# Prompt attention of a hybrid decoder: pairs in a new order, two sets of score buffers, and the second compression in two halves

## The chip, the cores and the metric

The kernel runs on one core of a Trainium2 chip. The metric is the device time of one execution in microseconds; the median of the runs is compared. The engines are TensorE (PE; PEld is its weight load), VectorE (DVE), ScalarE (ACT), GpSimd (POOL) and SyncE (SP); the last two mostly issue DMAs here. Each engine works through its own instructions in the order in which they are written, and waits at semaphores for the others.

## The reference, cut to what matters

Two layers of a decoder over 256 prompt tokens and 32 sample tokens (8 sequences of 4), all in f32. Each layer has three token mixers on one input projection; the change concerns the first, attention with three branches, for the prompt tokens. Keys of branch 0 are compressed: 32 positions of a stride of 16 are projected by weights `w_cmp`, for keys (kind 0) and values (kind 1).

```python
k_cmp = compress(strides[:, :, :, 0], w_halves[0])
v_cmp = compress(strides[:, :, :, 1], w_halves[1])
s_c = jnp.einsum('qgrd,cgd->qgrc', qi, k_cmp[b]) * scale      # branch 0: compressed
p_c = masked_softmax(s_c, ...);  o_c = jnp.einsum('qgrc,cgd->qgrd', p_c, v_cmp[b])
...                                                          # branch 1: selected blocks, branch 2: window, alike
o_nsa = jnp.einsum('bthk,btkhd->bthd', g_nsa, o_br)          # gated sum of the three
```

The sample tokens attend to 1024 past positions, whose rows lie in pages; these too are compressed, for the first four sequences (half 0) and the last four (half 1). After the mixers come the gated merge, an output projection, and in layer 0 a dense feed-forward network, in layer 1 a mixture of 8 experts.

## The kernel before

**Pairs.** The prompt's attention is cut into six pairs of a query tile qt (128 queries each) and a branch br. `pair_width` gives the keys: 15 for branch 0, 128 for the other branches of qt 0, and 256 for those of qt 1 (qt 1 sees both key tiles). I call a pair with 256 keys wide and the others slim. Each pair goes through the engines in this chain, for two key groups g:

- PE `pair_scores` (L633) makes the scores in PSUM, one bank for each g, two for a wide pair.
- DVE `pair_softmax` (L1573, L1577) scales and masks them into the score buffer `S_p[g]` in SBUF and takes the maximum.
- ACT `pair_exp` (L1333) takes the exponential in place, with the sum.
- DVE `pair_norm` (L1587 to L1592) multiplies by the gate over the sum.
- PE transposes (`pair_transposes`, L646), ACT copies the result from PSUM into `PT_p` (L1198, in `evac`) and gives a mark (`signal`, L1222).
- PE multiplies by the values (`pair_out`, L658), and DVE adds the result into `oN` (`pair_out`, L1600 to L1603), pair by pair.

There is one set of score buffers: `pair_softmax(m)` may write `S_p` only once the transposes of pair m-1 have read it (`filled(("T", l, m - 1, ...))`).

**What fills the chain's waits.** The input projection has 22 tiles that the attention doesn't need: `rest(i)` is one product of 8 blocks (L476), with an evacuation on ACT or DVE (kind x, c, b: a copy; z: Silu; h: a product on DVE). `PAIR_RESTS` puts nine of them, 3 to 11, between the steps of the pairs. A rest of kind z makes ACT load another function table than the exponential. `compress(1)`, the compression of half 1 of the sample's pages (L596, L603), stands in one piece before the scores of pair 3; ACT evacuates it (`evac_cmp`).

**Queues.** PSUM has 8 banks, taken in turn by every product (`bank`): PE waits until the use eight before has been evacuated. Weights come through a ring of 6 slots of 1 MB, 16 blocks each, which SP loads in the order in which PE uses them. The sample's pages are filled into three slots of `pages`, half by SP and half by POOL (`page_fill`, L435; windows of keys at L1096 and L1099), each fill when its slot's last reader is done (`frees`). PE waits in `compress` for both page fills of the half. After the pairs PE waits for `qbd`, the sample's queries spread out by DVE (L1642, L1645), and the sample's attention begins with the transposes at L681.

Of the kernel before, what the change touches and what calls it, by code (L numbers as in the profile page):

```python
# [39 lines left out]

CMP1_RESTS = 3
PAIRS = [(qt, br) for qt in range(2) for br in range(3)]
CMP1_PAIR = 2
PAIR_RESTS = [(3, 4), (5,), (6, 7), (8,), (9, 10), (11,)]

# [115 lines left out]
def build(nc, xT_in, consts, params, wstream, page_table, cmp_pages, slc_pages, win_kT, win_v, win_rows,  # L161
# [5 lines left out]
    with ExitStack() as ctx:  # L167
# [18 lines left out]
        mark = sb("mark", 2 * MARKS)  # L186
        REG = 11600
        reg = sb("phase_region", REG)
# [50 lines left out]
        rp = Region(scratch)  # L239
        S_p = [rp(1024), rp(1024)]  # L240
        PT_p = [rp(2, 4 * P), rp(2, 4 * P)]
        rs_ = Region(scratch)
        qbd = rs_(NB, 32)
        vc = rs_(HALF, P)
# [197 lines left out]
        def _(pe):  # L442
# [73 lines left out]
            for l in range(DEPTH):  # L516
# [40 lines left out]
                def rest(i):  # L557

                    product(("rest", l, i), KD, lambda k: xn[:, k, :])
# [13 lines left out]

                def compress(hf):

                    fills = [(l, hf, "cmp0"), (l, hf, "cmp1")]
                    for f in fills:
# [3 lines left out]
                        "p (n k j g c) -> p n k j g c", n=n, k=2, j=JP, g=NKV) for f, n in zip(fills, blocks_of)]  # L581
                    for kind in range(2):
                        out = [bank(("cmp", l, hf, kind, k)) for k in range(2)]
# [29 lines left out]
                for i in range(1, EARLY):  # L613
                    rest(i)
                compress(0)

# [21 lines left out]
                def pair_transposes(m):  # L638
                    w, nkc = pair_width(m)
                    for g in range(NKV):  # L640
                        s = S_p[g][:, 0:GRP * w * nkc].rearrange("p (r k) -> p r k", r=GRP)
# [546 lines left out]
        def _(act):  # L1188
# [56 lines left out]
            for l in range(DEPTH):  # L1245
# [81 lines left out]
                def pair_exp(m):  # L1327
                    w, nkc = pair_width(m)
                    for g in range(NKV):
                        s = S_p[g][:, 0:GRP * w * nkc].rearrange("p (r k) -> p r k", r=GRP)  # L1330
                        act.wait_ge(S["smax"], 12 * l + 2 * m + g + 1)
                        for r in range(GRP):
                            e = A.activation(s[:, r, :], s[:, r, :], ACT.Exp, bias=mx[:, g, r:r + 1],  # L1333
                                             accum_out=ssum[:, g, r:r + 1])
                        e.then_inc(S["exp_ready"], 1)

                pair_exp(0)
                for m in range(6):
                    w, nkc = pair_width(m)
                    if m == CMP1_PAIR:  # L1340
                        for kind, k in ((0, 0), (0, 1), (1, 0), (1, 1)):
                            evac_cmp(("cmp", l, 1, kind, k), kvT[1][kind][:, 2 * k:2 * k + 2, :])
                        signal("vcT_ready")
                    rest(PAIR_RESTS[m][0])
# [6 lines left out]
                    for i in PAIR_RESTS[m][1:]:  # L1351
                        rest(i)
# [128 lines left out]
        def _(dve):  # L1481
# [36 lines left out]
            for l in range(DEPTH):  # L1518
# [37 lines left out]
                def pair_softmax(m):  # L1556
# [9 lines left out]
                    for g in range(NKV):  # L1566
                        s = S_p[g][:, 0:GRP * w].rearrange("p (r k) -> p r k", r=GRP)
# [11 lines left out]
                def pair_norm(m):  # L1579
# [4 lines left out]
                    for g in range(NKV):  # L1584
                        s = S_p[g][:, 0:GRP * w].rearrange("p (r k) -> p r k", r=GRP)
                        dve.wait_ge(S["exp_ready"], 12 * l + 2 * m + g + 1)
                        link(V.reciprocal(rsum, ssum[:, g, :]))  # L1587
                        gate = gates[:, qt, g * 12:(g + 1) * 12].rearrange("p (r k) -> p r k", k=3)[:, :, br]
                        link(V.tensor_tensor(coef, rsum, gate, ALU.mult))
                        if br == 0:  # L1590
                            link(V.tensor_scalar(coef, coef, C("cmp_any")[:, qt:qt + 1], None, ALU.mult))
                        V.tensor_tensor(s, s, bc(coef, 2, w), ALU.mult).then_inc(S["norm_ready"], 1)  # L1592

                def pair_out(m):
# [3 lines left out]
                    dst = oN[:, :, qt * P:(qt + 1) * P]  # L1598
                    if br == 0:
                        V.tensor_copy(dst, src).then_inc(free(("O", l, m)), 1)  # L1600
                    else:
                        dve.wait_ge(*released(("O", l, m - 1)))
                        V.tensor_tensor(dst, dst, src, ALU.add).then_inc(free(("O", l, m)), 1)  # L1603
# [29 lines left out]
                for m in range(6):  # L1633
                    pair_norm(m)
                    rest(PAIR_RESTS[m][0])
                    if m < 5:
                        pair_softmax(m + 1)
                    for i in PAIR_RESTS[m][1:]:
                        rest(i)
                    pair_out(m)  # L1640

                link(V.memset(qbd, 0.0))  # L1642
                for g in range(NKV):
                    gd = slice(HD * g, HD * g + HD)
                    last = V.tensor_copy(qbd[gd, :, 16 * g:16 * g + 16].rearrange("p b (r t) -> p b r t", r=GRP),  # L1645
                                         qkv[gd, 0:GRP, TP:T].rearrange("p r (b t) -> p b r t", b=NB))
                last.then_inc(S["qbd_ready"], 1)
                for hf in range(2):
# [433 lines left out]
def weight_stream(a):  # L2082
# [9 lines left out]
    for l in range(DEPTH):  # L2092
# [10 lines left out]
        put(cm)  # L2103
        put(np.stack(rest[EARLY:EARLY + CMP1_RESTS]))
        put(cm)
        put(np.stack(rest[EARLY + CMP1_RESTS:]))
        mg = blocks(w[:, 4128:]).reshape(3, KD, KD, P, P)
# [127 lines left out]
```

## Time and profile before

| | |
|---|---|
| median of 3 runs | 2044.54 us (2044.1 to 2047.66) |
| the profiled execution | 2039.56 us, its span 2037.9 us |
| PE | busy 1973.1 us, 97% of the span |
| DVE, ACT, POOL | 463.2, 291.9 and 143.3 us |
| chain that ended last | PE 88%, issue 8%, DVE 2%, ACT 1%, DMA 1% |
| granted TensorE clock, mean | 0.991 |

PE is the engine to watch: what ends later on it ends the kernel later. The prompt's pairs run from 92.04 to 175.35 us in layer 0 and from 779.04 to 862.29 us in layer 1. The experts take the span's second part, from about 1150 us on, in which the DMA engines are nearly full. A busy PE is modelled: each matmul's shown end lies somewhat behind the start of the next, so that a row's length is longer than its place in the sequence.

### The profile page before, as it was taken

Reading aid. Unit: us, or ns where it says so; the run is one execution under the profiler, and the core shown is the slowest. Engines: PE = TensorE matmul, PEld = TensorE weight load, DVE = VectorE, ACT = ScalarE, POOL = GpSimd, SP = SyncE. Lnnn points to the kernel's source line nnn. Section 1 sums busy time; section 2 is a strip of 40 time slices with the busy share of each in tenths; the row PEclk is TensorE's granted clock in tenths of the full one; section 3 lists DMA queues with packets and bytes.
Section 4 is the critical chain, followed back from the end, with each engine's and each line's share of the span. In section 5 each row is a group of like instructions: output and inputs, shape, how many; then the busy total and the mean of one; then the engine's idle time right before and its main releaser. Section 6 shows DMA issues by size and latency. Waiting matters only on the chain.

```text
span 2037.9 us, 40320 instructions
## 1 busy us (share of the span) xinstructions
PE 1973.1 (97%) x17106; PEld 1418.3 (70%) x17106; DVE 463.2 (23%) x1189; ACT 291.9 (14%) x737; POOL 143.3 (7%) x246
## 2 busy tenths in 40 slices
PE   8998999999999999899999999999999999999996
PEld 6876677777777778667777556777767675646564
DVE  2334464310000132437442410010100100101011
ACT  2243222100000023512211200000000000000000
POOL 2210120000000010120000200000000000000000
PEclk9999999999999999999999999999999999999998
DMA  8853654364333264454233499999999999999996
GB/s 308 316 201 115 219 192 142 135 214 175 142 127 143 105 227 166 149 203 148 106 127 143 169 414 417 412 418 414 416 417 413 420 408 421 411 421 411 415 420 241
DMA packets 99833, 553.25 MB, mean 271 GB/s; under 512 B 13712, under 2 KB 30128, under 8 KB 40912
## 3 DMA queue, kind: packets, MB, share of 16 engines
q1 hardware_dynamic: 84144, 491.96, 61.1%
q0 software_dynamic: 12720, 48.97, 6.8%
q10 hardware_dynamic: 2800, 9.83, 1.4%
q8 instruction: 135, 2.21, 0.4%
q14 instruction: 34, 0.28, 0.0%
HBM read 532.08 MB, written 24.89 MB: 273 GB/s over the span
## 4 chain that ended last, share of the span: by engine, by line
PE 88%; issue 8%; DVE 2%; ACT 1%; DMA 1%; POOL 0%; DVEq 0%; POOLq 0%; SPq 0%; ACTq 0%
PE bank L476 42%; PE bank L966 35%; PE bank L603 3%; PE bank L633 1%; PE bank L658 1%; PE bank L742 1%; PE bank L720 1%; ACT phase_region L1198 0%; PE bank L786 0%; DVE phase_region L1573 0%; PE bank L854 0%; PE bank L933 0%; PE bank L646 0%; PE bank L495 0%; PE bank L487 0%
## 5 line engine op out<-in xcount | busy, mean ns | idle before, releaser
L966 PE MATMUL bank<-wring,phase_region 128*32 128x512 f32 (+2 forms) x10112 | 867.7, 506 | 1.0 <-DMA wring<-in_wstream 0.8
L966 PEld LDWEIGHTS bank<-wring,phase_region 128*32 128x32 f32 x10112 | 572.6, 110 | 296.0 <-issue 142.8
L476 PE MATMUL bank<-xn,wring 128*128 128x288 f32 x2496 | 631.5, 412 | 5.7 <-DVE phase_region L1573 3.6
L476 PEld LDWEIGHTS bank<-xn,wring 128*128 128x128 f32 x2496 | 473.1, 192 | 144.5 <-issue 12.7
L476 PE MATMUL bank<-phase_region,wring 128*128 128x288 f32 x608 | 148.2, 407 | 3.1 <-DVE mark L1494 2.5
L2046 DVE TENSOR_TENSOR tmp<-phase_region,bank 128x512 f32<-128x512 f32 (+1 forms) x48 | 28.6, 595 | 500.9 <-PE bank L966 500.9
L476 PEld LDWEIGHTS bank<-phase_region,wring 128*128 128x128 f32 x608 | 115.4, 190 | 36.0 <-DVE mark L1494 3.4
L1198 ACT ACTIVATE phase_region<-bank 128x512 f32<-128x512 f32 (+12 forms) x130 | 55.7, 469 | 411.7 <-PE bank L966 296.5
L1469 ACT ACTIVATE phase_region<-bank 128x512 f32<-128x512 f32 (+1 forms) x48 | 26.1, 544 | 531.6 <-PE bank L966 531.6
L2059 DVE COPY phase_region<-bank 32x256 f32<-32x256 f32 x32 | 13.5, 420 | 263.0 <-PE bank L966 262.7
L603 PE MATMUL bank<-pages,wring 128*64 128x128 f32 (+1 forms) x1024 | 58.9, 276 | 0.0
L603 PEld LDWEIGHTS bank<-pages,wring 128*64 128x64 f32 x1024 | 57.8, 137 | 0.0
L1174 POOL TENSOR_TENSOR turn<-turn 1x1 f32<-1x1 f32 x8 | 1.5, 183 | 678.8 <-DVE slot_row L2054 673.2
L1934 DVE TENSOR_TENSOR phase_region<-phase_region,bank 128x288 f32<-128x288 f32 x22 | 9.9, 454 | 158.7 <-PE bank L476 140.4
L435 POOL DMA_DIRECT2D pages<-in_slc_pages x64 | 34.3, 536 | 97.1 <-PE bank L603 68.7
L1573 DVE SCALAR_TENSOR_TENSOR phase_region<-bank,cst 128x512 f32<-128x512 f32 (+1 forms) x32 | 17.5, 567 | 100.3 <-PE bank L646 57.3
L435 POOL DMA_DIRECT2D pages<-in_cmp_pages x64 | 34.4, 538 | 58.1 <-issue 55.3
L1333 ACT ACTIVATE phase_region<-phase_region 128x15 f32<-128x15 f32 (+2 forms) x96 | 37.6, 392 | 3.1 <-DVE phase_region L1577 2.8
L1240 ACT ACTIVATE tmp<-xT 128x288 f32<-128x288 f32 x32 | 13.5, 440 | 160.3 <-DVE xT L1938 85.6
L1781 DVE TENSOR_TENSOR tmp<-bank,tmp 128x288 f32<-128x288 f32 x32 | 14.6, 457 | 90.4 <-PE bank L476 90.4
L1391 ACT ACTIVATE tmp<-bank 128x288 f32<-128x288 f32 x40 | 16.2, 409 | 123.6 <-PE bank L476 101.5
L1110 POOL DMA_DIRECT2D phase_region<-phase_region x16 | 7.9, 499 | 365.4 <-ACT phase_region L1255 365.4
(335 smaller groups left out, 1129.4 us busy)
## 6 DMA issues: line engine op xcount, KB each, us to landing
wring<-in_wstream SPq DMA_DIRECT2D x449, 1024.0 KB, 8.3
y_rows<-phase_region ACTq DMA_DIRECT2D x25, 384.0 KB, 7.5
pages<-in_cmp_pages POOLq DMA_DIRECT2D x64, 128.0 KB, 4.0
pages<-in_cmp_pages SPq DMA_DIRECT2D x64, 128.0 KB, 3.8
pages<-in_slc_pages SPq DMA_DIRECT2D x64, 128.0 KB, 4.4
pages<-in_slc_pages POOLq DMA_DIRECT2D x64, 128.0 KB, 4.5
out_win_keep<-in_win_rows POOLq DMA_DIRECT2D x2, 4064.0 KB, 26.4
pages<-in_win_kT POOLq DMA_DIRECT2D x4, 1024.0 KB, 5.3
```

The lines of the kernel that those rows point to most:

```text
L435: eng.dma_start(pages[:, at:at + 2 * P], src[bass.ds(page + l * n_pool, 1), :, :].rearrange("a p n -> (a p) n")).then_inc(fill_at[f][1], 16)
L476: mm = nc.tensor.matmul(ps[:, 0:width], wb, rhs(k), start=(k == 0), stop=(k == n - 1))
L603: mm = nc.tensor.matmul(ps[HD * g:HD * g + HD, 1 - a:1 - a + CPG * n].rearrange("p (n c) -> p n c", c=CPG), w, src[k][:, :, kind, jp, g, : ...
L633: mm = nc.tensor.matmul(ps[:, i * nk:(i + 1) * nk], qkv[gd, part * per + i, qt * P:qt * P + P], keys, start=True, stop=True)
L658: mm = nc.tensor.matmul(ps[gc, 0:512], v, PT_p[g][0:w, kc, :], start=(kc == 0), stop=(kc == nkc - 1))
L720: mm = nc.tensor.matmul(ps[32 * bi:32 * bi + 32, 0:512].rearrange("p (a b) -> p a b", a=4), qbd[:, hf * HALF + bi, :], kT[:, 4 * c:4 * c + ...
L742: nc.tensor.matmul(ps[32 * bi:32 * bi + 32, 0:P], PT_s[:, c, 32 * bi:32 * bi + 32], keys[bi][2][:, c, :], start=(c == 0), stop=False)
L966: mm = nc.tensor.matmul(ps[QT * q:QT * q + QT, out0:out0 + n], lhsT, wring[:, a:a + n], start=start, stop=stop)
L1198: return A.activation(out, in_, ACT.Copy)
L1333: e = A.activation(s[:, r, :], s[:, r, :], ACT.Exp, bias=mx[:, g, r:r + 1], accum_out=ssum[:, g, r:r + 1])
L1469: A.activation(sg[:, r % 3, 0:cols], psum[loop_bank(key)][:, 0:cols], ACT.Silu).then_inc(bank_free[loop_bank(key)], 1)
L2046: V.tensor_tensor(hq[r % 2][:, 0:cols], sg[:, r % 3, 0:cols], psum[b][:, 0:cols], ALU.mult).then_inc(bank_free[b], 1)
```

## The change

Four things change, all within the pairs of both layers. The order of the pairs becomes (0,0), (1,1), (0,1), (1,2), (0,2), (1,0) in (qt, br), so that pairs 1 and 3 are the wide ones. Even and odd pairs get score buffers of their own, `S_slim` and `S_wide`; `pair_softmax(m)` waits for the transposes of pair m-2. `compress(1)` is called once for each kind, behind the scores that follow pair 1's and pair 3's: kind 0 between the scores of pair 2 and the transposes of pair 1, kind 1 between the scores of pair 4 and the transposes of pair 3. There ACT takes the exponential of pair m+1 ahead of the evacuations, instead of behind them. The rests move to other places. `qbd` gets room of its own and is made after pair 0's output instead of after pair 5's. The order of the weight stream follows PE's.

```diff
-        S_p = [rp(1024), rp(1024)]
+        S_wide = [rp(1024), rp(1024)]
+        S_slim = [rp(512), rp(512)]
...
-PAIRS = [(qt, br) for qt in range(2) for br in range(3)]
-CMP1_PAIR = 2
-PAIR_RESTS = [(3, 4), (5,), (6, 7), (8,), (9, 10), (11,)]
+PAIRS = [(0, 0), (1, 1), (0, 1), (1, 2), (0, 2), (1, 0)]
+CMP1_KIND = {1: 0, 3: 1}
+BEFORE_T = [(3,), (), (), (), (8,), (10,)]
+BEFORE_O = [(4,), (5,), (6,), (7,), (9,), (11,)]
...
+        def S_p(m):
+            return S_wide if m % 2 else S_slim
...
                 for m in range(6):
-                    if m == CMP1_PAIR:
-                        compress(1)
                     if m < 5:
                         pair_scores(m + 1)
-                    rest(PAIR_RESTS[m][0])
+                    if m in CMP1_KIND:
+                        compress(1, (CMP1_KIND[m],))
+                    for i in BEFORE_T[m]:
+                        rest(i)
                     pair_transposes(m)
-                    for i in PAIR_RESTS[m][1:]:
+                    for i in BEFORE_O[m]:
                         rest(i)
                     pair_out(m)
...
-                    if m == CMP1_PAIR:
-                        for kind, k in ((0, 0), (0, 1), (1, 0), (1, 1)):
+                    if m in CMP1_KIND:
+                        pair_exp(m + 1)
+                        kind = CMP1_KIND[m]
+                        for k in range(2):
                             evac_cmp(("cmp", l, 1, kind, k), kvT[1][kind][:, 2 * k:2 * k + 2, :])
-                        signal("vcT_ready")
+                        if kind == 1:
+                            signal("vcT_ready")
...
-                    if m < 5:
+                    if m < 5 and m not in CMP1_KIND:
                         pair_exp(m + 1)
...
-                        if m:
-                            dve.wait_ge(*filled(("T", l, m - 1, g, pair_width(m - 1)[1] - 1)))
+                        if m > 1:
+                            dve.wait_ge(*filled(("T", l, m - 2, g, pair_width(m - 2)[1] - 1)))
...
                     pair_out(m)
+                    if m == 0:
+                        link(V.memset(qbd, 0.0))
```

**PE, the wide pairs before.** These are the scores of pair 4 to the last product of pair 5. L633 are scores (128x256: a wide pair), L476 a rest, L646 transposes (15x128: of a pair with 15 keys), L658 the product with the values, L681 the sample's first transposes.

```order
L633 MATMUL bank<-phase_region 128x256 x8
L476 MATMUL bank<-xn,wring 128x288 x8
L646 MATMUL bank<-cst,phase_region 15x128 x8
L658 MATMUL bank<-phase_region 64x512 x2
L633 MATMUL bank<-phase_region 128x256 x8
L476 MATMUL bank<-xn,wring 128x288 x8
L646 MATMUL bank<-cst,phase_region 128x128 x16
L476 MATMUL bank<-xn,wring 128x288 x8
L658 MATMUL bank<-phase_region 64x512 x4
L476 MATMUL bank<-xn,wring 128x288 x8
L646 MATMUL bank<-cst,phase_region 128x128 x16
L658 MATMUL bank<-phase_region 64x512 x4
```

Now PE has this from pair 1's scores to pair 2's output; L638 are the scores, L601 and L608 one kind of the compression, L651 transposes, L481 a rest and L663 the product with the values.

```order
L638 MATMUL bank<-phase_region 128x256 x8
L481 MATMUL bank<-xn,wring 128x288 x8
L651 MATMUL bank<-cst,phase_region 15x128 x8
L481 MATMUL bank<-xn,wring 128x288 x8
L663 MATMUL bank<-phase_region 64x512 x2
L638 MATMUL bank<-phase_region 128x128 x8
L601 MATMUL bank<-cst,wring 64x129 x4
L608 MATMUL bank<-pages,wring 64x128 x64
L651 MATMUL bank<-cst,phase_region 128x128 x16
L481 MATMUL bank<-xn,wring 128x288 x8
L663 MATMUL bank<-phase_region 64x512 x4
L638 MATMUL bank<-phase_region 128x256 x8
```

Between a wide pair's scores and its transposes stood one rest; now a slim pair's scores and half the compression stand there too. Between the first wide pair's output and the next transposes (those of slim pair 2) stand the scores of pair 3 alone. The first half of the compression begins one rest, one slim transpose and one slim output earlier than the whole did.

**ACT, the end of the pairs before**, from the Silu of the last rest of kind z (L1297) to the exponential of the sample's compressed scores (L1361):

```order
L1297 ACT_TABLE_LOAD
L1297 ACTIVATE o_ssm<-bank 128x288
L1198 ACTIVATE phase_region<-bank 128x512 x4
L1222 ACTIVATE mark<-cst 1x1
L1333 ACT_TABLE_LOAD
L1333 ACTIVATE phase_region<-phase_region 128x256 x8
L1198 ACTIVATE phase_region<-bank 128x288
L1198 ACTIVATE phase_region<-bank 128x512 x4
L1222 ACTIVATE mark<-cst 1x1
L1198 ACTIVATE phase_region<-bank 63x512
L1222 ACTIVATE mark<-cst 1x1
L1361 ACTIVATE phase_region<-phase_region 128x63
```

And now (L1303 is the Silu, L1371 the exponential):

```order
L1303 ACT_TABLE_LOAD
L1303 ACTIVATE o_ssm<-bank 128x288
L1204 ACTIVATE phase_region<-bank 128x288
L1204 ACTIVATE phase_region<-bank 15x512 x2
L1228 ACTIVATE mark<-cst 1x1
L1204 ACTIVATE phase_region<-bank 63x512
L1228 ACTIVATE mark<-cst 1x1
L1371 ACT_TABLE_LOAD
L1371 ACTIVATE phase_region<-phase_region 128x63
```

The last Silu stands behind the last pair's exponential, and a table load stands ahead of the exponential of the sample's scores.

## Rows read from the trace of the kernel before

**Rows 1.** PE's waits, whole span: what waited, for whom, us in total, times, longest.
```profile
PE bank L658 <- ACT mark L1222: 5.0, 6, 0.9
PE bank L476 <- DVE phase_region L1573: 3.6, 2, 1.8
PE bank L681 <- DVE phase_region L1645: 3.1, 2, 1.6
PE bank L633 <- DVE phase_region L1573: 2.0, 2, 1.0
PE bank L646 <- DVE phase_region L1573: 0.7, 2, 0.3
```
**Rows 2.** Timeline of PE, layer 0: start us, us, instructions, idle before.
```profile
104.48 1.07 PE L658 MATMUL bank<-phase_region 15*64 15x512 f32 x4
105.48 1.16 PE L633 MATMUL bank<-phase_region 64*128 64x128 f32 x16
...
133.26 1.04 PE L646 MATMUL bank<-cst,phase_region 128*128 128x128 f32 x8
134.14 4.05 PE L476 MATMUL bank<-xn,wring 128*128 128x288 f32 x16
...
139.12 2.00 PE L633 MATMUL bank<-phase_region 64*128 64x256 f32 x16
```
**Rows 3.** Timeline of DVE, layer 0, pair 0's output and pair 1's norm.
```profile
105.60 0.69 DVE L1600 COPY o_nsa<-bank 128x512 f32<-128x512 f32 x1 [2.61 <-PE bank L658]
106.21 0.17 DVE L1587 RECIPROCAL phase_region<-phase_region 128x4 f32<-128x4 f32 x1
...
107.22 0.17 DVE L1587 RECIPROCAL phase_region<-phase_region 128x4 f32<-128x4 f32 x1
```
**Rows 4.** Timeline of DVE, layer 0: wide pair 4's first softmax step and last norm step.
```profile
145.67 1.29 DVE L1573 SCALAR_TENSOR_TENSOR phase_region<-bank,cst 128x512 f32<-128x512 f32 x2 [4.14 <-PE bank L646]
...
153.22 1.23 DVE L1592 TENSOR_TENSOR phase_region<-phase_region 128x1024 f32<-128x1024 f32 x1
```
**Rows 5.** Timeline of PE: one kind of the compression (layer 0), pair 0's output (layer 1).
```profile
113.76 7.15 PE L603 MATMUL bank<-pages,wring 128*64 128x128 f32 x128
...
789.86 1.07 PE L658 MATMUL bank<-phase_region 15*64 15x512 f32 x4
```
**Rows 6.** SP's page loads of half 1, layers 0 and 1; landing time of the last.
```profile
92.88 12.16 SPq L435 DMA_DIRECT2D pages<-in_cmp_pages  x16
...
DMA to landing us min/median/max: 6.0/6.0/6.0
...
779.35 9.59 SPq L435 DMA_DIRECT2D pages<-in_cmp_pages  x16
...
DMA to landing us min/median/max: 3.4/3.9/4.5
```
**Rows 7.** Stretches: us, busy PE, PEld, DVE, ACT, POOL, granted clock, DMA share, GB/s.
```profile
156.00:160.00 4.00, 1.86 (x12) 1.23 (x10) 3.93 (x6) 3.67 (x9) 0.00 (x0) 1.00 0.00 0
...
832.00:836.00 4.00, 2.73 (x12) 1.72 (x14) 3.93 (x6) 3.58 (x11) 0.00 (x0) 0.76 0.30 119
...
1200.00:2038.00 838.00, 817.48 (x9608) 553.48 (x9600) 83.31 (x160) 35.06 (x62) 27.71 (x36) 0.99 0.99 405
```
**Rows 8.** Timeline of PE, layer 1: a wide pair's scores at the lower clock.
```profile
834.34 3.54 PE L633 MATMUL bank<-phase_region 64*128 64x256 f32 x16 [1.00 <-DVE phase_region L1573]
```
**Rows 9.** Timeline, layer 0: an ACT table load; DVE's sample probabilities, and their reader on PE.
```profile
128.77 1.28 ACT L1297 ACT_TABLE_LOAD   x1
...
177.50 0.26 DVE L1659 TENSOR_SCALAR phase_region<-phase_region 128x63 f32<-128x63 f32 x1
...
180.17 0.33 PE L692 MATMUL bank<-phase_region,cst 128*128 128x63 f32 x2
```
**Rows 10.** Timeline, layer 0: POOL's page loads of the selected blocks, their first reader.
```profile
128.81 9.32 POOL L435 DMA_DIRECT2D pages<-in_slc_pages  x16 [35.11 <-PE bank L603]
...
192.34 1.92 PE L720 MATMUL bank<-pages,phase_region 128*32 128x512 f32 x16
```

More of the change, by code:

```diff
@@ L186, in build @@
         mark = sb("mark", 2 * MARKS)
-        REG = 11600
+        REG = 11600 + 1280
         reg = sb("phase_region", REG)
@@ L239, in build @@
         rp = Region(scratch)
-        S_p = [rp(1024), rp(1024)]
+        S_wide = [rp(1024), rp(1024)]
+        S_slim = [rp(512), rp(512)]
         PT_p = [rp(2, 4 * P), rp(2, 4 * P)]
+        qbd = rp(NB, 32)
         rs_ = Region(scratch)
-        qbd = rs_(NB, 32)
         vc = rs_(HALF, P)
@@ L572, in _, with compress @@
                     nc.tensor.matmul(ps[:, 0:7 * TQ], C("spread")[:, P * r:P * r + P], qk_std, start=True, stop=True).then_inc(done, 1)
-                def compress(hf):
+                def compress(hf, kinds):
                     fills = [(l, hf, "cmp0"), (l, hf, "cmp1")]
@@ L581, in compress @@
                         "p (n k j g c) -> p n k j g c", n=n, k=2, j=JP, g=NKV) for f, n in zip(fills, blocks_of)]
-                    for kind in range(2):
+                    for kind in kinds:
                         out = [bank(("cmp", l, hf, kind, k)) for k in range(2)]
@@ L614, in _ @@
                     rest(i)
-                compress(0)
+                compress(0, (0, 1))
                 pe.wait_ge(S["vcT_ready"], 3 * l + 2)
@@ L1339, in _ @@
                     w, nkc = pair_width(m)
-                    if m == CMP1_PAIR:
-                        for kind, k in ((0, 0), (0, 1), (1, 0), (1, 1)):
+                    if m in CMP1_KIND:
+                        pair_exp(m + 1)
+                        kind = CMP1_KIND[m]
+                        for k in range(2):
                             evac_cmp(("cmp", l, 1, kind, k), kvT[1][kind][:, 2 * k:2 * k + 2, :])
-                        signal("vcT_ready")
-                    rest(PAIR_RESTS[m][0])
+                        if kind == 1:
+                            signal("vcT_ready")
+                    for i in BEFORE_T[m]:
+                        rest(i)
                     for g in range(NKV):
@@ L1348, in _ @@
                     signal("pt_ready")
-                    if m < 5:
+                    if m < 5 and m not in CMP1_KIND:
                         pair_exp(m + 1)
-                    for i in PAIR_RESTS[m][1:]:
+                    for i in BEFORE_O[m]:
                         rest(i)
@@ L1634, in _ @@
                     pair_norm(m)
-                    rest(PAIR_RESTS[m][0])
+                    for i in BEFORE_T[m]:
+                        rest(i)
                     if m < 5:
                         pair_softmax(m + 1)
-                    for i in PAIR_RESTS[m][1:]:
+                    for i in BEFORE_O[m]:
                         rest(i)
                     pair_out(m)
[L1642 to L1647, printed above, removed]
+                    if m == 0:
+                        link(V.memset(qbd, 0.0))
+                        for g in range(NKV):
+                            gd = slice(HD * g, HD * g + HD)
+                            last = V.tensor_copy(qbd[gd, :, 16 * g:16 * g + 16].rearrange("p b (r t) -> p b r t", r=GRP),
+                                                 qkv[gd, 0:GRP, TP:T].rearrange("p r (b t) -> p b r t", b=NB))
+                        last.then_inc(S["qbd_ready"], 1)
                 for hf in range(2):
@@ L2103, in weight_stream @@
         put(cm)
-        put(np.stack(rest[EARLY:EARLY + CMP1_RESTS]))
-        put(cm)
-        put(np.stack(rest[EARLY + CMP1_RESTS:]))
+        put(np.stack(rest[3:5]))
+        put(cm[0])
+        put(np.stack(rest[5:7]))
+        put(cm[1])
+        put(np.stack(rest[7:]))
         mg = blocks(w[:, 4128:]).reshape(3, KD, KD, P, P)
```

13 lines of the change are left out of this document (6 added, 7 removed).

## The prediction

> **What bounds the kernel now.** The page comes first: PE is busy 97% of the span and makes 88% of the chain that ended last. The change can gain only what PE waits, so PE's waits are read next [rows 1]. Five groups of them lie within the pairs and add up to 5.0 + 3.6 + 3.1 + 2.0 + 0.7 = 14.4 us, 7.2 in each layer. They are three things. L658 waits for ACT's mark: a pair's transposes are done and ACT still copies them, with no rest in between. L633, L476 and L646 wait for DVE at L1573: the scores of wide pair 5 can't leave PSUM, because the one set of score buffers still holds pair 4, and the products behind them find no free bank. L681 waits for L1645: the sample's queries are laid out only behind pair 5's output.
>
> A row's length overstates a group's place in the sequence, so a shown wait is too short. Slim transposes are shown at 1.04 us, and the next group starts 0.88 after them; an output is shown at 1.07, and the next starts 1.00 after it [rows 2]. Each layer has seven waits (the counts of rows 1, halved). Five follow transposes, or a part of them, and hide 0.16 each; two follow outputs and hide 0.07: 7.2 + 0.8 + 0.14 = 8.1 us of real waiting a layer.
>
> **The change part by part.** PE's instructions stay the same in number and shape; only waits change.
>
> *Removed.* The three outputs that waited for ACT's mark now have a rest of 4 us [rows 2] between transposes and output. The waits at pair 5 go: each wide pair is followed by a slim one with its own buffer. Do the wide pairs find their norm done in time? In the trace a wide pair's whole chain, from DVE's first softmax step to its last norm step, takes from 145.67 to 154.45 us, 8.8 us [rows 4]. In the new order, from the end of pair 3's scores PE passes slim transposes 0.9, rest 4, output 1.0, slim scores 1.1 and a kind of the compression of over 7.15 us [rows 2, 5] before it wants that norm: 14 us. DVE starts on pair 3 some 1 us late, behind pair 2's norm, and has pair 2's output in between: 3 us or more remain. Pair 1 has 4 + 0.9 + 4 + 1 + 1.1 + 7.2 = 18. The wait for `qbd` goes too, since DVE makes it at pair 0, where DVE idles. I let all of it go: 8.1 x 2 = 16.3 us (unrounded).
>
> *Added, behind pair 1's output.* On DVE the output of pair 1 stands ahead of pair 2's norm, and PE has only pair 3's scores between that output and pair 2's transposes. DVE starts 0.12 us after PE's output step ends (105.48 to 105.60), takes 0.61 for the output and 1.01 for each key group's norm [rows 2, 3]. With 0.12 again for the way back, the second group is ready after 2.87 us. PE wants it after wide scores, 1.93, and half the transposes, 0.44 [rows 2]: 2.37. A new wait of 0.5 us a layer, 1.0 together. Its bounds are 0 and the 1.8 us of the longest wait for DVE in the pairs [rows 1], 3.6 together.
>
> *Added, the pages.* `compress` waits for both page fills of its half, whichever kind it is called for. Pair 0's output will begin 0.84 us later than it did, since wide scores stand where slim ones did (2.00 against 1.16), and behind it come 1.0 of output and 1.1 of scores: 104.48 + 0.84 + 2.1 = 107.4 us in layer 0 [rows 2]. SP issues the last page at 92.88 + 12.16 - 0.3 = 104.7 us, and it lands 6.0 later, at 110.7 [rows 6]. The fill's start depends on the compression of half 0, ahead of all that changes, so it won't come earlier: PE waits 3.3 us. In layer 1 the same sum is 789.86 + 0.84 + 2.1 = 792.8 [rows 5]; the last page is issued at 788.6 and lands 4.5 later, at 793.1 [rows 6]: 0.3 us. Together 3.6. Bounds: 0.7, if the last page of layer 0 lands after the 3.4 us of the quickest row; 7.7, if layer 1's fill takes the 17.8 us from first issue to landing that layer 0's does (779.4 + 17.8 = 797.2, a wait of 4.4). I take each layer's own rows.
>
> *Hidden.* The pages of the selected blocks are loaded when kind 1 is done, some 14 us later than before: from 143 instead of 128.8 us in layer 0. POOL issues them in 9.3 us and with 6.0 to land they are there at 158; their first reader came at 192.34 and comes 4 us earlier now, so 29 us of PE's work covers them [rows 6, 10]. The weight ring is six slots ahead, and PE's waits in the layers name no weight. One more table load, 1.28 us, stands ahead of the sample's first exponential and delays the probabilities by at most that: they were there at 177.76 and PE asked at 180.17 [rows 9]; of 2.4 us of cover 1.1 is left. Without that cover it would cost 1.28 a layer.
>
> The Trainium skill speaks against this part. "ScalarE: Activation LUTs", section "What ACT_TABLE_LOAD costs", puts a change of tables at 2.66 us, a load and a drain. The trace shows the load at 1.28, and whether a drain comes with it no row here shows. By the page the cover is overrun by some 0.2 us a layer, and the sum would be 0.4 smaller.
>
> *The clock.* The granted clock falls to the lower level (1.2 instead of 2.4 GHz) for a few us at a time: the mean is 0.76 in 832 to 836 us [rows 7]. This fall stands among the waits that go, and it made a wide pair's scores last 3.54 us in place of 2.00 [rows 8, 2]: 1.5 us. I take it as gone, and one new fall of that price as put in its place behind the 3.3 us wait for pages: nothing in the sum, with 1.5 us of gain and 3 of loss as bounds.
>
> **Sum.** 16.3 - 1.0 - 3.6 = 11.7 us less. The profiled span of 2037.9 becomes 2026.2, and its execution of 2039.56 becomes 2027.9. The median of the runs lies 5 us above the profiled execution; the difference carries over: 2044.5 - 11.7 = **2032.8 us**, 0.57% less.
>
> **The rivals.**
>
> *The pages land in time.* The waits for pages shrink to 0.5 us and the fall at 832 goes without a new one. For it: landing times within one fill go from 3.4 to 6.0 us, so they depend on what else is moving. Against: layer 0's fill was at 110.7. 16.3 - 1.0 - 0.5 + 1.5 = 16.3: 2028.2 us. Chance 0.15.
>
> *The pages are late in both layers and the clock falls behind the waits.* 7.7 us of waiting, and 2.3 net of falls, between one and two: 16.3 - 1.0 - 7.7 - 2.3 = 5.3: 2039.2 us. For it: PE now gets to the pages some 6 us earlier in each layer, and layer 0's fill is that slow. Against: layer 1's own rows. The clock's part: PE was busy for 2.73 of 4 us where it fell, and for only 1.86 of 4 in 156 to 160, where it stayed at 1.00 [rows 7], so a wait brings a fall at times. Chance 0.22.
>
> Beside it stands "TensorE: Matmul & The Clock Gate" of the Trainium skill, Part 1: the lower level is the default, and activity lifts it. By that rule the 3.3 us wait brings a fall for certain; the stretch from 156 us shows that not every wait does.
>
> *The gain stops at the experts.* From 1200 us on the DMA share is 0.99 [rows 7]. If the weight stream set the end on a schedule of its own, an earlier PE would meet an empty ring: 2044.5 us. Against: the ring is full when the stage begins, and each load waits for a slot that PE frees, so the stream moves with PE. Chance 0.07.
>
> *Slower: the compression runs at the lower clock.* One place, the first matmuls behind the wait for pages: the clock falls there and stays down through a whole kind, whose 7.4 us become 14.8. In both layers that costs 14.8 against a gain of 11.7: 2047.6 us. It decides from the point where the lower level lasts 11.7 us a layer, since PE does half its work in it. Against: a fall cost 1.5 us here, a fifth of that. Chance 0.03.
>
> *It does less than it says.* A wait behind one of the in-order queues, DVE's or ACT's, that following the chain has missed takes back 8 of the 11.7 us, half of what was removed. For it: the covers are thin, 3 us at pair 3 and 1 at the table load. 2040.8 us. Chance 0.08.
>
> **How the numbers follow.** The forecast, 2032.8, has 0.45, with a range of its own from 2030 to 2036. The whole range goes from 2027, a little below the early pages, to 2040, a little above the late ones: 0.45 + 0.15 + 0.22 = 0.82. A difference of 0.2%, 4.1 us, is about what a measurement of this kernel can tell from none; that line lies at 2040.4. Faster has the forecast's 0.45, 0.15, 0.20 of the late pages and 0.02 of the last rival, 0.82. Within 0.2% are the experts' 0.07, 0.06 of the last rival and the late pages' other 0.02, with 0.01 of the slower case lying close: 0.15 rounded. Slower: 0.03.
>
> **What would show it.** In the changed kernel's trace: no wait for ACT's mark at the pairs' outputs, none for the softmax at scores, none at the sample's first transposes (now L687); one of 0.5 us before pair 2's transposes, for DVE's norm; one at half 1's first compression matmul (L601), near 3.3 us in layer 0 and 0.3 in layer 1. From pair 0's scores to L687 it was 83.3 us in either layer. It should be 79 in layer 0, or 80.5 with a new fall behind the wait, and 74.4 in layer 1. The experts' stage should be as long as it was. The prediction is wrong if pages land elsewhere than these rows say, if any other wait of over 1 us stands in the pairs, or if falls of the clock come more than once more or less often.

## The result, and the profile after

The changed kernel takes 2028.59 us (median of 6 runs, 2025.08 to 2031.56) against 2044.32 for the kernel before; the ratio is 0.9932, with a 95% interval from 0.9919 to 0.9946. That is 13.9 us less (11.0 to 16.6). The ratio compares fast runs alone, so one execution of the kernel before, at 3011.71 us, is not in it, and the plain medians lie 15.7 us apart. A second series, on another chip, gave 0.9940 (0.9923 to 0.9957), 12.3 us. The forecast was 2032.8 us, 11.7 less, in a range from 2027 to 2040. The gain of 11.7 lies within both intervals.

PE's waits in the changed kernel, whole span (what waited, for whom, us in total, times, longest):

```profile
PE bank L601 <- issue: 3.5, 2, 3.0
...
PE bank L638 <- ACT mark L1228: 1.1, 2, 0.6
PE bank L624 <- ACT mark L1228: 1.0, 2, 0.5
...
PE bank L651 <- DVE phase_region L1602: 0.6, 2, 0.3
```

Nothing is left of [rows 1]: outputs (now L663) no longer wait for ACT's mark, scores and rests not for the softmax, and the sample's first transposes (L687) for nothing. Two new entries stand in their place, L601 and L651, both at the places that the prediction names. L624 and L638 stand ahead of the pairs (L638 at pair 0's first scores); the kernel before has both too, as long.

The timeline of PE around the first of the two, in layer 0, and in layer 1 (start us, us, instructions, idle before):

```profile
105.59 1.07 PE L663 MATMUL bank<-phase_region 15*64 15x512 f32 x4
106.59 1.16 PE L638 MATMUL bank<-phase_region 64*128 64x128 f32 x16
110.71 1.13 PE L601 MATMUL bank<-cst,wring 128*64 128x129 f32 x8 [2.96 <-issue]
111.59 8.20 PE L608 MATMUL bank<-pages,wring 128*64 128x128 f32 x128
...
129.30 0.66 PE L651 MATMUL bank<-cst,phase_region 128*128 128x128 f32 x4
130.26 0.66 PE L651 MATMUL bank<-cst,phase_region 128*128 128x128 f32 x4 [0.30 <-DVE phase_region L1602]
...
791.93 1.16 PE L638 MATMUL bank<-phase_region 64*128 64x128 f32 x16
793.59 0.67 PE L601 MATMUL bank<-cst,wring 128*64 128x129 f32 x8 [0.50 <-issue]
```

The wait at L601 is put down to "issue", since the profile finds no engine that released it. SP's page loads name the cause. These are SP's loads of half 1 in the changed kernel, then the last of them in layer 0 with its time to landing:

```profile
93.12 12.59 SPq L440 DMA_DIRECT2D pages<-in_cmp_pages  x16
...
L440 SPq DMA_DIRECT2D pages<-in_cmp_pages x1: 333/333/333, 105.4 to 105.4; - x1
...
DMA to landing us min/median/max: 5.2/5.2/5.2
```

105.4 + 5.2 = 110.6, and PE goes on at 110.71. Behind the wait the clock is down: L601 lasts 1.13 us where it lasts 0.67 in layer 1, L608 8.20 against 7.15 [rows 5]. Granted clock is the third column from the end in these stretches of the changed kernel:

```profile
108.00:112.00 4.00, 1.29 (x12) 1.32 (x14) 3.81 (x8) 0.00 (x0) 0.00 (x0) 0.78 0.69 272
112.00:116.00 4.00, 4.00 (x62) 4.00 (x60) 1.97 (x3) 3.19 (x16) 0.00 (x0) 0.79 0.02 8
116.00:120.00 4.00, 4.00 (x72) 3.83 (x69) 0.00 (x0) 0.39 (x2) 0.00 (x0) 1.00 0.01 4
```

I call stage the stretch from pair 0's first score to the sample's first transposes. It was 83.3 us in both layers. It is now 172.74 - 92.25 = 80.5 in layer 0 and 854.19 - 779.27 = 74.9 in layer 1: 11.1 us less in sum. PE's instructions are the same, and the falls of the clock nearly cancel: the one at 832 us (1.5) is gone, one behind the wait for pages (1.4) has come, and the one at pair 0's scores in layer 0 is in both profiles. So the 11.1 us are waits.

### The profile page after: what moved, and what is told of

Same layout as the page of the kernel before. It is cut to its first block, busy times and chain, and to the rows that moved or that the text cites. A ratio compares the mean times of both kernels' runs of the same rounds, so it can differ in the third digit from the quotient of the medians.

```text
span 2029.9 us, 40318 instructions
## 1 busy us (share of the span) xinstructions
PE 1974.8 (97%) x17106; PEld 1417.1 (70%) x17106; DVE 462.1 (23%) x1189; ACT 291.7 (14%) x737; POOL 143.2 (7%) x246
## 4 chain that ended last, share of the span: by engine, by line
PE 89%; issue 8%; DVE 2%; DMA 1%; ACT 1%; POOL 0%; DVEq 0%; POOLq 0%; SPq 0%; ACTq 0%
PE bank L481 42%; PE bank L972 36%; PE bank L608 3%; PE bank L663 1%; PE bank L651 1%; PE bank L638 1%; PE bank L726 1%; PE bank L748 1%; PE bank L939 0%; PE bank L792 0%; PE bank L860 0%; PE bank L500 0%; PE bank L492 0%; PE bank L577 0%; PE bank L739 0%
## 5 line engine op out<-in xcount | busy, mean ns | idle before, releaser
L972 PE MATMUL bank<-wring,phase_region 128*32 128x512 f32 (+3 forms) x10112 | 868.0, 506 | 1.0 <-DMA wring<-in_wstream 1.0
L481 PE MATMUL bank<-xn,wring 128*128 128x288 f32 x2496 | 630.4, 411 | 2.1 <-DVE xn L1523 2.1
L481 PEld LDWEIGHTS bank<-xn,wring 128*128 128x128 f32 x2496 | 472.7, 192 | 139.5 <-issue 11.9
L481 PE MATMUL bank<-phase_region,wring 128*128 128x288 f32 x608 | 148.2, 407 | 3.1 <-DVE mark L1504 2.5
L481 PEld LDWEIGHTS bank<-phase_region,wring 128*128 128x128 f32 x608 | 115.3, 190 | 36.0 <-DVE mark L1504 3.4
L608 PE MATMUL bank<-pages,wring 128*64 128x128 f32 (+1 forms) x1024 | 60.0, 279 | 0.0
L608 PEld LDWEIGHTS bank<-pages,wring 128*64 128x64 f32 x1024 | 59.0, 139 | 0.0
L481 PE MATMUL bank<-o_nsa,wring 128*128 128x288 f32 x128 | 32.4, 406 | 0.0
```

The costliest lines, as they stand in the source:

```text
L481: mm = nc.tensor.matmul(ps[:, 0:width], wb, rhs(k), start=(k == 0), stop=(k == n - 1))
L608: mm = nc.tensor.matmul(ps[HD * g:HD * g + HD, 1 - a:1 - a + CPG * n].rearrange("p (n c) -> p n c", c=CPG), w, src[k][:, :, kind, jp, g, : ...
L972: mm = nc.tensor.matmul(ps[QT * q:QT * q + QT, out0:out0 + n], lhsT, wring[:, a:a + n], start=start, stop=stop)
```

## Experiments

The stage in both layers, from each kernel's profile, and the timed runs:

| kernel | stage, layer 0 | layer 1 | median us | ratio to before (95%) |
|---|---|---|---|---|
| before | 83.3 | 83.3 | 2044.3 | |
| changed | 80.5 | 74.9 | 2028.6 | 0.9932 (0.9919 to 0.9946) |
| e1, queries early | 81.6 | 84.6 | 2038.1 | 0.9980 (0.9968 to 0.9991) |
| e7, two buffers | 79.5 | 79.5 | 2033.8 | 0.9955 (0.9941 to 0.9970) |
| e2, one piece | 82.2 | 76.3 | 2035.7 | 0.9964 (0.9945 to 0.9983) |
| e3, one-buffer wait | 87.3 | 82.2 | 2043.9 | 1.0004 (0.9988 to 1.0020) |
| e4, windows later | 74.5 | 74.4 | 2023.1 | 0.9893 (0.9866 to 0.9920) |
| e5, norm first | 81.9 | 73.9 | 2026.7 | 0.9907 (0.9881 to 0.9934) |
| e6, both | 75.5 | 73.8 | 2022.2 | 0.9886 (0.9865 to 0.9906) |
| e8, pages later | 86.4 | 82.8 | 2042.0 | 0.9987 (0.9973 to 1.0000) |
| e9, changed again | 82.7 | 74.9 | 2029.9 | 0.9940 (0.9923 to 0.9957) |
| e10, windows later, old order | 83.3 | 83.2 | 2041.0 | 0.9995 (0.9980 to 1.0010) |
| e11, both again | 75.5 | 73.8 | 2023.2 | 0.9906 (0.9890 to 0.9922) |

A stage is good to 0.1 us except for falls of the clock, of 1.4 to 3 us each, which come or don't. So parts are read from the waits in the trace, and the timed runs say how large the whole is. e1, e7, e2 and e3 ran beside the kernel before on one chip, e4, e5, e6 and e8 on a second, e9 to e11 on a third; the kernel before took 2043.8, 2045.1 and 2043.4 us there. The ratios are to these. Experiments are compared with the changed kernel across chips by their ratios, which is good to some 4 us. An edit that adds lines moves the line numbers behind it by two or three: L601 is L603 in e8.

### One part of the change at a time, on the kernel before

**e1_queries_early.**

```diff
+        qbd = rp(NB, 32)
         rs_ = Region(scratch)
-        qbd = rs_(NB, 32)
...
                     pair_out(m)
+                    if m == 0:
+                        link(V.memset(qbd, 0.0))
```

> The kernel before, with one part of the change: the sample's queries (qbd) get room of their own and are made behind pair 0's output. Theory (three separate causes of waiting, each a term of its own): the wait of 1.55 us ahead of the sample's first transposes goes in both layers and no other changes, so from the first score (L633) to the sample's first transposes it is 81.7 us in place of 83.3 where falls of the clock are the same, and the whole is 3.2 us shorter. Rival (DVE is late at pair 5 anyway, and the wait moves one step on): the stage keeps its length within 0.3 us, with a new wait of 1 to 1.5 us at the sample's first scores or probabilities.

Measured: the wait of 1.55 us at L681 is gone in both layers and no other has come:

```profile
171.82 1.94 PE L658 MATMUL bank<-phase_region 128*64 128x512 f32 x8 [0.89 <-ACT mark L1222]
173.69 0.65 PE L681 MATMUL bank<-cst,phase_region 128*63 128x128 f32 x4
```

The rival falls. The stage shows it badly: pair 5's scores are at the lower clock in both layers (3.49 and 3.79 us where 2.00 is the length at full clock; before, in layer 1 alone), and in layer 1 the two rests behind them are slowed too (5.31 and 5.72 us for 4.15). The runs give 4.1 us less (1.8 to 6.5), with 3.2 expected.

**e7_two_buffers.** The old order with two full sets of buffers; pair 0's compressed values `vcp` move to a free part of `oC_` for room.

```diff
-        S_p = [rp(1024), rp(1024)]
+        S_sets = [[rp(1024), rp(1024)], [rp(1024), rp(1024)]]
...
-                        if m:
-                            dve.wait_ge(*filled(("T", l, m - 1, g, pair_width(m - 1)[1] - 1)))
+                        if m > 1:
+                            dve.wait_ge(*filled(("T", l, m - 2, g, pair_width(m - 2)[1] - 1)))
```

> The kernel before, with another part alone: two sets of score buffers used in turn (both wide; pair 0's compressed values move to a free part of another tensor to make room), while order of the pairs, rests and compression stay as they were. Theory (buffers alone are worth little without the order, because in the old order two wide pairs follow each other and DVE can't take pair 5's scores before it has ended pair 4's norm): the waits at pair 5's scores and in pair 4's transposes go (1.07 + 0.5 us), the one at the rest behind them stays at 1.3 of 1.95 us, the waits for ACT's copies and for qbd stay: about 2.2 us a layer, 4.4 in all. Rival (the buffer was the whole cause of the waits for DVE): 3.5 us a layer, 7 in all, and no wait for the softmax left.

Measured, PE's waits over the whole span:

```profile
PE bank L661 <- ACT mark L1225: 5.0, 6, 0.9
...
PE bank L684 <- DVE phase_region L1648: 3.1, 2, 1.6
...
PE bank L479 <- DVE phase_region L1576: 2.5, 2, 1.2
```

The waits at scores and in the transposes are gone, and the rest behind them still waits 1.24 us a layer for the softmax: buffers alone remove 2.2 of the 3.5 us, because DVE still has two wide pairs in a row. Both stages are 79.5 us, free of falls: 81.7 (83.3 less a fall of 1.6) minus 2.2. The runs gained more than that, 9.2 us (6.1 to 12.1) against 4.4 expected. The stages account for 7.5 of it, 4.4 by waits and 3.1 by the two falls that the profile of before had in them; whether the falls went because of the edit isn't shown. That DVE's row of wide pairs keeps the rest of the wait is read from the order of the program; no run takes it apart.

### One part undone, on the changed kernel

**e2_one_piece.**

```diff
-CMP1_KIND = {1: 0, 3: 1}
+CMP1_KIND = {1: (0, 1)}
```

> The changed kernel with the second compression in one piece again, both kinds behind pair 2's scores (the order of the weights follows it). Theory (each wide pair needs some 7 us of work beside its rest, and one kind of the compression is what covers it): pair 3 loses its cover; PE waits about 1.5 + 0.7 us for DVE's norm at pair 3's transposes and 1.8 us for ACT's mark at its output, so the stage is 4.0 us longer a layer than in the changed kernel and the whole 8 us slower than that. Rival (the buffers and the rests do the work, and where the compression stands is nearly free): under 1 us a layer.

Measured, layer 0 at pair 3 (layer 1 the same within 0.01):

```profile
142.28 1.16 PE L638 MATMUL bank<-phase_region 64*128 64x128 f32 x16
144.69 1.09 PE L651 MATMUL bank<-cst,phase_region 128*128 128x128 f32 x8 [1.24 <-DVE phase_region L1601]
146.23 1.09 PE L651 MATMUL bank<-cst,phase_region 128*128 128x128 f32 x8 [0.45 <-DVE phase_region L1601]
```

Pair 3 does lose its cover, and its norm comes 1.4 and 0.6 us too late, which is what was expected for the transposes. The third wait, 1.8 us at its output, didn't come: `CMP1_KIND` also steers where ACT takes the next exponential, so with the edit pair 4's exponential went back behind pair 3's copies and left them undisturbed. So this run undoes two things, and prices the division at 2.0 us a layer, not 4.0. The rival (under 1) falls as well. The stages are longer by less, 1.7 and 1.4 us, since the waits for pages were shorter here (2.6 and 0.1 us). By the ratios the run is 6.5 us slower than the changed kernel, with 8 expected; the 3.4 us between that and the 3.1 of the stages are within what such comparisons are good for.

**e3_one_buffer_wait.**

```diff
-                        if m > 1:
-                            dve.wait_ge(*filled(("T", l, m - 2, g, pair_width(m - 2)[1] - 1)))
+                        if m:
+                            dve.wait_ge(*filled(("T", l, m - 1, g, pair_width(m - 1)[1] - 1)))
```

> The changed kernel with the own buffers undone in effect: the softmax of pair m waits again for the transposes of pair m-1, all else as changed. Theory (the new order needs the second set, since now the exponential of the slim pair stands on ACT ahead of the wide pair's copies and comes late): a new wait of some 2.4 us for ACT's mark at the outputs of pairs 1 and 3 and 0.2 at the rests ahead of them, 5.2 us a layer, so the whole is 10.4 us slower than the changed kernel and only some 3 us faster than the one before. Rival (the order alone gives the gain, the buffers are dispensable): under 1 us a layer.

Measured, PE's waits (whole span), and the two outputs in layer 0:

```profile
PE bank L663 <- ACT mark L1228: 8.6, 4, 2.2
...
128.54 1.94 PE L663 MATMUL bank<-phase_region 128*64 128x512 f32 x8 [2.10 <-ACT mark L1228]
...
155.66 3.60 PE L663 MATMUL bank<-phase_region 128*64 128x512 f32 x8 [2.19 <-ACT mark L1228]
```

The waits are where they were expected, 4.6 us a layer with the hidden 0.16 each (5.2 expected), and the second is followed by a fall (3.60 against 1.94), in layer 1 both are. The stages are 6.9 and 7.2 us longer than in the changed kernel. By the ratios the run is 14.7 us slower than that, with 10.4 expected, and the whole gain is gone. In this order the second set of buffers isn't an extra: without it the order is worth nothing.

### The wait for pages

**e4_windows_later.**

```diff
+                if hf == 0:
+                    pool.wait_ge(*fill_at[(l, 1, "cmp1")][1:])
                 at = page_slot(f)
```

> The changed kernel with one wait more on POOL: the loads of the sample's window keys and values (2 MB) of half 0 are issued only when the second page fill of half 1 has landed, so that they don't share the DMA engines with it. Theory (the 3.0 us wait ahead of the compression in layer 0 is for pages that come late because the DMA engines are full): the fill is then bound by SP's issue, 16 pages of 0.55 us, lands by 106 us, ahead of PE's 107.7, and the wait is gone in layer 0, and the 0.5 us in layer 1 too: 3.5 us less than the changed kernel, and 1.5 us more where a fall of the clock stood behind that wait. Rival (the fill is slow for another reason, the weight load of 1 MB ahead of it or SP's issue): the last page still lands after 109 us and at most 1 us is gained.

Measured, layer 0: SP's page loads, the landing times of the 16, and PE at the compression.

```profile
91.86 8.85 SPq L440 DMA_DIRECT2D pages<-in_cmp_pages  x16
...
DMA to landing us min/median/max: 2.9/3.7/4.6
...
103.81 1.16 PE L638 MATMUL bank<-phase_region 64*128 64x128 f32 x16
105.06 0.67 PE L601 MATMUL bank<-cst,wring 128*64 128x129 f32 x8
105.53 7.18 PE L608 MATMUL bank<-pages,wring 128*64 128x128 f32 x128
```

The last load is issued at 100.4 and lands by 105.0, 13.1 us from the start of the fill instead of 17.5, and PE starts the compression at 105.06, 1.25 us after the scores where 1.09 is the step without a wait. Not only the landing got quicker: SP took 8.85 us to issue the 16 loads in place of 12.59, so the window loads slow SP's issue too. The wait and the fall behind it are gone, and layer 0's stage is at 74.5, the fall at pair 0 being absent too. That settles the cause; the rival falls. By the ratios the run is 8 us faster than the changed kernel, where 5 were expected.

**e8_pages_later**, the opposite:

```diff
+                if n0 == 0 and f[1:] == (1, "cmp1"):
+                    eng.wait_ge(*fill_at[(l, 0, "win")][1:])
```

> The opposite of the windows behind the pages: SP issues the second page fill of half 1 only when the window loads of half 0 have landed. Theory (PE waits for pages, and a fall of the clock follows such a wait when it is long): the last page lands some 5 to 8 us later, near 117 us in layer 0 and 800 in layer 1, PE waits 9 and 7 us at the compression's first matmul, and a fall of 1.5 us follows in both layers: 13 + 1.5 us slower than the changed kernel, about as slow as the one before. Rival (falls come by chance, whatever PE waited): as slow by the waits alone, 12 to 13 us, with the clock at 1.00 behind at least one of the two.

Measured, PE in both layers:

```profile
116.17 1.13 PE L603 MATMUL bank<-cst,wring 128*64 128x129 f32 x8 [9.85 <-issue]
117.05 8.91 PE L610 MATMUL bank<-pages,wring 128*64 128x128 f32 x128
...
802.74 1.13 PE L603 MATMUL bank<-cst,wring 128*64 128x129 f32 x8 [6.48 <-issue]
803.63 8.67 PE L610 MATMUL bank<-pages,wring 128*64 128x128 f32 x128
```

The clock is down behind both waits. The rival, falls by chance, has nothing for it here. The waits grew by 12.9 us in sum, the stages by 13.8, and the runs by 11 (ratio 0.9987 against 0.9932), with 14.5 expected. Of the stages the forecast missed that the fall in layer 0 was there already and that the one at pair 0 (2.89 us for the first scores, 4.58 in the changed kernel) was not; the 3 us between stages and runs are within what two chips differ by.

**e10_windows_later_old**, e4's edit on the kernel before:

> The kernel before with the windows loaded behind the pages, nothing else. Theory (the kernel before came to the pages at 113.3 us, after they had landed at 110.7, so their landing time was hidden): no difference to the kernel before within 2 us, and the last page landed by 107 us. Rival (the full DMA engines slow PE or others in that stretch by themselves): 3 us or more faster.

Measured: SP issued the loads in 8.46 us from 94.51 on, the last landed by 107.1, and both stages kept their length (83.3 and 83.2). The runs differ by 1 us (0.9980 to 1.0010); by themselves they would leave room for the 3 us of the rival, the stages don't. So the window loads cost nothing until the change brought PE to the pages 6 us earlier.

### The wait for the norm, and both together

**e5_norm_first.**

```diff
                     pair_norm(m)
+                    if m == 2:
+                        pair_out(1)
...
-                    pair_out(m)
+                    if m != 1:
+                        pair_out(m)
```

> The changed kernel with two steps of DVE exchanged: pair 2's norm ahead of pair 1's output. Theory: the wait of 0.3 us shown (0.5 real) within pair 2's transposes goes in both layers, the stage is 0.5 us shorter a layer, 1 us in all, too little for the timed runs and read from the trace. Rival (the norm is late because of pair 2's exponential, not of the output): the wait stays.

Measured: the wait at L651 is gone in both layers, and layer 1's stage is 73.9 us, 1.0 less than in the changed kernel: 0.5 for the norm, and 0.5 since in that execution the pages were in time. Layer 0 had its wait for pages (3.46 us) and a longer fall behind it (L608 9.64 us). The timed difference, 2 us to the changed kernel's first series, is within what series differ by, so the 1 us of this edit is shown by the traces alone.

**e6_both** has the edits of e4 and e5; **e11_both_again** is the same kernel, beside **e9_changed_again**, the changed kernel as it is.

> The changed kernel with both: windows loaded behind the pages, and pair 2's norm ahead of pair 1's output. Theory: all waits within the pairs are gone, from the first score to the sample's first transposes 73.6 us in either layer where the clock stays up (80.5 and 74.9 in the changed kernel), and the whole is 4.5 us faster than the changed kernel, 6 with the fall behind the pages gone. Rival (what PE gains it gives back in falls of the clock elsewhere): the stage is shorter by that but the whole by less than 2 us.

> The changed kernel as it is, beside the next two and the kernel before on one chip. Theory (the stage of the pairs is deterministic but for falls of the clock, and what differs between executions lies in falls): again 2.5 to 3.5 us of waiting for pages in layer 0 with a fall right behind it, 0.2 to 0.6 us in layer 1, and a ratio to the kernel before between 0.9925 and 0.9945. Rival (the profile of the changed kernel was an unlucky one and the wait for pages is not always there): under 1.5 us of waiting in layer 0.

> The changed kernel with windows behind the pages and pair 2's norm ahead of pair 1's output, once more, beside the changed kernel on the same chip. Theory: 4.5 us (waits of 3.5 and 1.0) to 6 us (with the fall behind the pages) faster than the changed kernel; stage 73.8 us in either layer but for a fall ahead of it. Rival (the difference between the two jobs came from the chips): under 3 us.

Measured: no wait within the pairs in either profile of both edits. Layer 1's stage is 73.8 us twice; layer 0's 75.5 twice, each with the fall at pair 0's scores that e4 lacks. The changed kernel again waited for pages, 3.80 us in layer 0, somewhat above the 2.5 to 3.5 expected, with a fall behind it (L608 9.60 us) and 0.47 in layer 1. Side by side on one chip the medians are 2023.15 and 2029.92 us, 6.8 us apart, where 4.5 to 6 were expected. This version beats both kernels: 0.9906 of the kernel before (0.9890 to 0.9922), on the other chip 0.9886.

## Why the prediction was right, and where it wasn't

**The waits that go.** Right in all: 8.1 us a layer. Layer 1 gives the sum back: its stage lost 8.3 us, of which 1.5 are the fall that went, while 0.6 and 0.5 of new waits and 0.2 of the compression in two parts (15.2 us for both kinds, 15.0 before) were added. Parts are now priced apart: the early queries 1.6 (e1), buffers in the old order 2.2 (e7). The remaining 4.3 went with the new order, its rests and the divided compression, of which the division is 2.0 (e2). No run has the rests' new places alone, so that they took the waits for ACT's mark is read from the program and not tested by itself.

**The covers.** At pair 3, said to have 3 us or more, DVE's norm is ready by 139.6 and PE asks at 144.4: 4.8 us. At the table load, said to have 1.1, the probabilities are there by 176.3 and PE comes at 177.55: 1.2 us. No wait has come at either. The rows of ACT at the sample's first exponential in the changed kernel:

```profile
173.92 0.19 ACT L1228 ACTIVATE mark<-cst 1x1 f32<-1x1 f32 x1
174.12 1.28 ACT L1371 ACT_TABLE_LOAD   x1
175.42 0.35 ACT L1371 ACTIVATE phase_region<-phase_region 128x63 f32<-128x63 f32 x1
```

The exponential starts 1.30 us after the load: of the drain that "ScalarE: Activation LUTs" of the Trainium skill adds (2.66 us for load and drain, section "What ACT_TABLE_LOAD costs") nothing is seen, with ACT idle. The measurement decides, and the term of 0.4 us stays out.

**The new wait on DVE.** 0.5 us a layer forecast. The halves of the transposes start 0.96 us apart (129.30 to 130.26) where 0.44 is their step: 0.52. e5 shows the cause, DVE's order.

**The pages.** Forecast: landed at 110.7 and 793.1, waits of 3.3 and 0.3. Measured: 110.6 and 793.5, waits of 3.0 and 0.5 as shown, in the second profile 3.8 and 0.5. The bound of 7.7 for two late fills, and with it the rival of late pages, overstated layer 1.

**The clock.** The fall at 832 us is gone, and one came behind the wait for pages, as counted. The rival put "between one and two" falls behind such waits; every one of the seven waits of 2.6 us and more at the compression (changed, e2, e3, e5, e9, and e8 twice) had one behind it. For the shorter waits in the pairs of before they came at times only. "TensorE: Matmul & The Clock Gate" of the Trainium skill, Part 1, has the lower level as the default, lifted by activity. The seven waits agree with it; that a wait brings a fall "for certain" was the prediction's own step, and the shorter waits speak against it.

**From one profiled execution to the median.** The stages should have lost 4.3 and 8.9 us less a new fall, 11.7; they lost 2.8 and 8.3. The missing 0.5 are in layer 1, 0.3 at the pages and 0.2 in the divided compression. Of these 11.1 us the whole profiled span shows 8.0 (2037.9 to 2029.9, with 2026.2 forecast). By the starts of the same groups in both profiles, 0.2 are lost ahead of the pairs and 2.8 between the two stages, where the changed kernel has falls at 200 and at 420 to 460 us and the kernel before has none. The 1.6 won back at 900 us, where only the kernel before has a fall, are lost again by 1150.

The median went the other way: 2028.6, 4.2 us below the forecast. The term that was off is the clock's, "nothing in the sum": it was counted in a profile that wasn't typical. In the three later series the kernel before has a mean granted clock of 0.989 or less in 39 of 60 executions, with spans from 2040.6 us up, and of 0.991 or 0.992 in 21, with spans up to 2039.5. The profiled one, 2037.9 at 0.991, belongs to the second group; the median lies in the first, and that is where the 5 us between them come from. The changed kernel, in all of its 12 executions, is at 0.990 to 0.993. So the typical execution of before has more falls than the one whose falls were counted, and the changed kernel has fewer of them than that. The timed gains are 2.8 and 1.2 us more than the stages' 11.1, too little to be told from noise by themselves; which falls went is open, since only single executions have a trace. It is luck that 2028.6 is all but the 2028.2 of the rival with the pages in time: the waits for pages were there.

**The other rivals.** The gain didn't stop at the experts: it is there in the runs, and the experts' group has the same busy time as before (868.0 us, 867.7 before). Nothing was slower. Pages in time is what e4 makes of the kernel: 2023.1 us, where that rival had 2028.2. It had the right sign and place; the 5 us more are no waits that it named, and where they lie isn't shown beyond the fall at pair 0 that e4's profile lacks.

## What to carry to other kernels

When an engine gets to some step earlier than it used to, look up when that step's data land: here page loads that had landed 2.6 us before PE asked for them came to cost 3.6 us of waiting, a quarter of the gain, and holding another, unhurried transfer behind them gave that back. On engines that work in order, long and short work in turn went with a second set of buffers: buffers alone were worth a quarter of the removed waits, and the order without the buffers nothing. Each of the seven waits of 2.6 us and more at the compression cost 1.4 to 2.9 us beyond its length, since the clock fell behind it. Before the falls in one profile are priced, the mean clock of many executions shows whether that profile is a typical one.

## What the runs showed of the hardware

- DMA traffic from another queue slows the issue itself, not the landing alone. In layer 0, SP's 16 page loads took 12.1 to 13.9 us to issue while POOL's 2 MB of windows were moving, and 8.5 to 8.9 without them (e4, e6, e10, e11, and e8, where the windows come first); the slowest landing went from 8 us and more to 4.6 or less. In layer 1 the issue hardly differs (9.2 to 9.9 us with, 8.2 to 9.4 without); why isn't shown.
- Falls of TensorE's clock behind the waits for pages cost 1.4 to 2.1 us, and 2.8 to 2.9 in two cases (L608 9.6 us in place of 7.15, L601 1.13 in place of 0.67). Falls come at other places with the same instructions, even far from the edit.
- The executions of one kernel differ by 1.5 to 14 us within a series, those of the kernel before in step with the mean granted clock: spans of 2037.7 us on average at 0.991 and 0.992, 2043.1 at 0.988, 2048.7 at 0.985.
